# A two-layer decoder step on one core: prompt attention weights divided before their transposition, one search's counts split over two engines, and a reversed block order

## The reference, cut to what matters

```python
# mixer A: logits of the selected keys, softmax, values (16 heads of 64 in 2 groups)
logits = q @ k_sel * HEAD_DIM ** -0.5 + bias
p = softmax(where(dist >= 0, logits, NEG));  o = p @ v_sel
# mixer B: the sink joins the maximum and the sum, not the values
m = maximum(max(logits), sink);  e = exp(logits - m)
p = e / (sum(e) + exp(sink - m)); o = p @ v
```

## Time and profile before

| | us |
|---|---|
| median of 3 runs (lowest to highest) | 2345.16 (2342.01 to 2346.71) |
| the profiled execution, its own time | 2343.02 |
| its span in the profile | 2341.2 |
| mixer A's prompt attention, first logits to the first instruction of the samples | 131.89 |
| mixer B's prompt attention, the same | 80.70 |

### The profile page before, as it was taken

The page is one execution under the profiler, slowest core; times in us unless marked ns, Lnnn a source line. Parts: engine busy times, 40 slices in busy tenths (PEclk is TensorE's granted clock), DMA queues, the critical chain, the costliest instruction groups (busy, mean ns, idle before and its releaser), DMA issues.

```text
span 2341.2 us, 39794 instructions
## 1 busy us (share of the span) xinstructions
PE 2258.6 (96%) x14801; PEld 2029.8 (87%) x14819; DVE 1137.1 (49%) x1811; ACT 415.4 (18%) x848; POOL 1029.7 (44%) x622
## 2 busy tenths in 40 slices
PE   7999999999888899999999999999999999999997
PEld 6999989959666588999999999999996689999997
DVE  4544522488584546555512555542264465555311
ACT  3101000131554412010000101000015420101002
POOL 4546455414001024555555555555541055555552
PEclk9999999999799999999999999999999899999998
DMA  5435363535003433333223333322350023333221
GB/s 125 99 73 115 78 155 89 114 64 147 10 1 100 130 89 77 86 81 81 78 84 90 82 86 85 81 78 82 94 154 23 1 73 81 81 86 83 79 83 60
DMA packets 378042, 196.33 MB, mean 84 GB/s; under 512 B 66531, under 2 KB 374476, under 8 KB 377932
## 3 DMA queue, kind: packets, MB, share of 16 engines
q1 hardware_dynamic: 366108, 180.79, 31.3%
q10 hardware_dynamic: 11552, 13.71, 2.0%
q0 software_dynamic: 288, 0.56, 0.1%
HBM read 192.23 MB, written 11.64 MB: 87 GB/s over the span
## 4 chain that ended last, share of the span: by engine, by line
PE 61%; DVE 2%; ACTq 0%; ACT 0%; issue 0%; DVEq 0%
PE psum L594 17%; PE psum L597 11%; PE psum L595 10%; PE psum L593 10%; PE psum L596 9%; PE psum L749 1%; PE psum L775 1%; DVE XS L1448 1%; PE psum L745 1%; PE psum L789 1%; ACTq L1200 0%; PE psum L758 0%; DVE squares L1481 0%; PE psum L939 0%; PE psum L938 0%
## 5 line engine op out<-in xcount | busy, mean ns | idle before, releaser
L545 POOL CAST WSP<-WST 128x1024 fp32r<-128x1024 f32 (+1 forms) x305 | 310.5, 1018 | 1250.0 <-PE psum L597 1008.8
L547 POOL TENSOR_TENSOR WSP<-WST,WSP 128x1024 fp32r<-128x1024 f32 (+1 forms) x305 | 709.3, 2326 | 24.5
L594 PE MATMUL psum<-XS,WSP 128*128 128x512 f32 x1672 | 658.4, 394 | 0.0
L593 PE MATMUL psum<-XS,WSP 128*128 128x320 f32 x1672 | 520.4, 311 | 9.5 <-DVE XS L1448 4.3
L597 PE MATMUL psum<-XS,WSP 128*128 128x320 f32 x1672 | 522.7, 313 | 0.0
L595 PE MATMUL psum<-XS,WSP 128*128 128x320 f32 x1672 | 519.2, 311 | 0.0
L596 PE MATMUL psum<-XS,WSP 128*128 128x256 f32 x1672 | 474.0, 283 | 0.0
L596 PEld LDWEIGHTS psum<-XS,WSP 128*128 128x128 f32 x1672 | 314.8, 188 | 71.5
L593 PEld LDWEIGHTS psum<-XS,WSP 128*128 128x128 f32 x1672 | 321.4, 192 | 11.6 <-DVE XS L1448 5.2
L597 PEld LDWEIGHTS psum<-XS,WSP 128*128 128x128 f32 x1672 | 321.5, 192 | 0.0
L594 PEld LDWEIGHTS psum<-XS,WSP 128*128 128x128 f32 x1672 | 314.4, 188 | 0.4
(11 more groups left out here) (325 smaller groups left out, 2595.0 us busy)
## 6 DMA issues: line engine op xcount, KB each, us to landing
WST<-in_ffn_w_gate SPq DMA_DIRECT2D x168, 256.0 KB, 3.9
WST<-in_ffn_w_up SPq DMA_DIRECT2D x168, 256.0 KB, 3.9
WST<-in_ffn_w_down SPq DMA_DIRECT2D x192, 224.0 KB, 3.5
WST<-in_a_w_in SPq DMA_DIRECT2D x28, 256.0 KB, 4.4
kv0A<-in_cache_kv SPq DMA_DIRECT2D x48, 128.0 KB, 2.3
kv2A<-in_cache_kv SPq DMA_DIRECT2D x48, 128.0 KB, 2.3
WST<-in_b_w_in SPq DMA_DIRECT2D x20, 256.0 KB, 4.0
kscr<-in_cache_idx SPq DMA_DIRECT2D x128, 32.0 KB, 2.1
```

Source lines behind the costliest of these rows:

```text
L545: nc.gpsimd.tensor_copy(WSP[s][:, 0, 0:width], WST[s][:, 0:width]).then_inc(w_hi, 1)
L547: nc.gpsimd.tensor_tensor(WSP[s][:, 1, 0:width], WST[s][:, 0:width], WSP[s][:, 0, 0:width].bitcast(F32), ALU.subtract).then_inc(w_split, 1)
L593: mm(front, high, x[:, 0, 0:FRONT], start=first, stop=False)
L594: mm(split, high, x[:, :, FRONT:TOK], start=first, stop=False)
```

## The change

1. Both mixers: the weights are divided before T. VectorE's new `factors(u)` takes the reciprocal of the unit's two row sums and multiplies the weights in place, one instruction for each n; T waits for that (`pn_set`) and no longer for E. `row_scales`, `scales`, `products` and `otok` are gone. The high and low part come straight from the PSUM banks (`high_part` on ScalarE, `low_part` on VectorE).
2. TensorE's order in unit u was T(u), L(u+2), V(u-1); it is now L(u+2), V(u-1), T(u).
3. Mixer B: the sink is now a column of the bias strip (and a second column that holds the mask), so that maximum and sum take it in; strips are 258 wide for 256, and the four small sink instructions go.
4. Mixer A's blocks run 3, 2, 1, 0.
5. Of the counts beside the loop, those of even units below 24 are ScalarE's and the others VectorE's. Before, units 0 to 8 had ScalarE's and 9 to 23 VectorE's.
6. `block_diagonal` of mixer A goes from VectorE to GpSimd, ahead of its long wait; GpSimd's next weight split waits for the last `factors` (`pn_set`), before for the last logits. In the samples' part `new_logits` comes after three `keys`, and mixer B's samples wait for `ot_evac` later.

The core of the diff (the strips' widths, the removed buffers and names are left out):

```diff
@@ TensorE
-                for u, (r, i, g) in enumerate(units):
-                    more = u + 2 < len(units)
-                    transposed(u)
-                    if g == GRP - 1:
-                        row_scales(r, i)
-                    elif more:
-                        logits(u + 2)
-                    if u:
-                        values(u - 1)
-                    if g == GRP - 1 and more:
-                        logits(u + 2)
+                for u in range(len(units)):
+                    if u + 2 < len(units):
+                        logits(u + 2)
+                    if u:
+                        values(u - 1)
+                    transposed(u)
...
-                        pe.wait_ge(ms["p_set"], 2 * u + n + 1)
+                        pe.wait_ge(ms["pn_set"], 2 * u + n + 1)
@@ ScalarE
-                if FOUND + 1 + u <= SIGN_COUNTS:
+                if u in SIGN_UNITS:
                     count(FOUND + 1 + u)
...
+                    if g == 5:
+                        high_part(r, 0)
+                    if g == 1 and r:
+                        high_part(r - 1, 1)
@@ VectorE
+                def factors(u):
+                    r, i, g = units[u]
+                    dve.wait_ge(ms["p_set"], 2 * (u + 1))
+                    nc.vector.reciprocal(m["ri"][:, i, :, g], m["rs"][:, i, :, g]).then_inc(ms["ri_set"], 1)
+                    dve.wait_ge(ms["ri_set"], u + 1)
+                    for n in range(KVH):
+                        p = m["p"][:, u % 2, n, 0:key_range(L, i)[1]]
+                        ts(p, p, m["ri"][:, i, n, g:g + 1], None, ALU.mult).then_inc(ms["pn_set"], 1)
...
+                    nc.vector.tensor_reduce(m["nm"][:, i, :, g], PS[u % 2][:, :, 0:nk], AX, ALU.max, negate=True)\
+                        .then_inc(ms["nm_set"], 1)
+                    if u:
+                        factors(u - 1)
+                    if g == 7:
+                        low_part(r, 0)
                     if g == 3 and r:
-                        parts(r - 1)
+                        low_part(r - 1, 1)
                     after(u)
@@ constants
-ORDER = {"A": (0, 1, 2, 3), "B": (3, 2, 1, 0)}
-BITS, SIGN_COUNTS, FOUND = 32, 16, 7
+SINK = {"A": 0, "B": 2}
+STRIP = {L: 2 * P + SINK[L] for L in "AB"}
+ORDER = {"A": (3, 2, 1, 0), "B": (3, 2, 1, 0)}
+BITS, FOUND, SIGN_UNITS = 32, 7, range(0, 24, 2)
```

More of the change, by code:

```diff
@@ L557, in ffn, with block_diagonal @@
                         split(n0 + GU_CHUNKS + q, i, RING, DB * P)
+            def block_diagonal(m, ms):
+                pool.wait_ge(acc_evac, at["inA"][1] + A_CHUNKS + RING)
+                nc.gpsimd.memset(m["qbd"][:, :, :], 0.0).then_inc(ms["qbd_clear"], 1)
+                pool.wait_ge(ms["qbd_clear"], 1)
+                for n in range(KVH):
+                    h = slice(n * HD, (n + 1) * HD)
+                    dst = m["qbd"][h].rearrange("p b (n g t) -> p n g b t", n=KVH, g=GRP)[:, n]
+                    nc.gpsimd.tensor_copy(dst, m["qT"][h, :, SEQ:TOK].rearrange("p g (b t) -> p g b t", b=NB))\
+                        .then_inc(ms["qbd_set"], 1)
+                pool.wait_ge(ms["qbd_set"], KVH)
             ffn("ffn0")
@@ L569, in _ @@
                 .then_inc(MS["A"]["selb_in"], 16)
-            pool.wait_ge(MS["A"]["qk_ps"], NQT * GRP)
+            m, ms = mixers["A"], MS["A"]
+            block_diagonal(m, ms)
+            pool.wait_ge(MS["A"]["pn_set"], 2 * NQT * GRP)
             for t in range(ND):
@@ L751, in logits @@
                     ins.then_inc(ms["qk_ps"], 1)
[L753 to L761, removed]
                 turned = turned_counts(L)
@@ L883, in paged_sample_attention @@
                 keys(0, 2)
+                new_logits()
                 logits(0, 0)
@@ L1593, in prompt_attention @@
                         between(r)
-                    if g in (1, 2) and r:
-                        products(r - 1, (g - 1,))
-                    k0, nk = key_range(L, i)
+                    nk = key_range(L, i)[1] + SINK[L]
                     dve.wait_ge(ms["qk_ps"], u + 1)
-                    nm = m["nm"][:, i, :, g]
-                    ins = nc.vector.tensor_reduce(nm, PS[u % 2][:, :, 0:nk], AX, ALU.max, negate=True)
-                    if L == "B":
-                        steps.done(ins)
-                        ins = tt(nm, nm, m["nsink"][:, :, g], ALU.min)
-                    ins.then_inc(ms["nm_set"], 1)
-                    if L == "B" and g == GRP - 1:
-                        dve.wait_ge(ms["nm_set"], u + 1)
-                        if r:
-                            dve.wait_ge(ms["es_set"], r)
-                        tt(m["es"][:, :, :], m["nm"][:, i], m["nsink"][:, :, :], ALU.subtract).then_inc(ms["es_in"], 1)
-                    if g == 0 and r:
-                        row_scales(r - 1)
+                    nc.vector.tensor_reduce(m["nm"][:, i, :, g], PS[u % 2][:, :, 0:nk], AX, ALU.max, negate=True)\
[4 more added lines that the diff above has]
+                        low_part(r, 0)
                     if g == 3 and r:
-                        parts(r - 1)
+                        low_part(r - 1, 1)
                     after(u)
-                row_scales(NQT - 1)
-                products(NQT - 1, (0, 1))
-                parts(NQT - 1)
+                factors(len(units) - 1)
+                low_part(NQT - 1, 1)
             def paged_sample_attention(m, ms):
@@ L1906, in selections @@
                     sample_mask()
-                elif k == BITS + 2:
-                    block_diagonal(m, ms, a0 + A_CHUNKS)
             ranks = squares.rearrange("p a t -> p (a t)")[:, 0:SEGW]
@@ L2002 @@
 KV_SLOTS = 3
-ORDER = {"A": (0, 1, 2, 3), "B": (3, 2, 1, 0)}
-BITS, SIGN_COUNTS, FOUND = 32, 16, 7
+SINK = {"A": 0, "B": 2}
+STRIP = {L: 2 * P + SINK[L] for L in "AB"}
+ORDER = {"A": (3, 2, 1, 0), "B": (3, 2, 1, 0)}
+BITS, FOUND, SIGN_UNITS = 32, 7, range(0, 24, 2)
+SIGNED = (*range(1, FOUND + 1), *(FOUND + 1 + u for u in SIGN_UNITS))
 HALF_B = NB // 2
```

99 lines of the change are left out of this document (31 added, 68 removed).

## The result

The change makes the step slower: 2362.85 us (median of 4 runs, 2360.04 to 2367.29) against 2343.59 in the same comparison, a ratio of 1.0082 (95% interval 1.0061 to 1.0103), so 19 us more. The forecast was 2357, slower, with a range of 2341 to 2366. The two profiled executions, 2343.02 and 2360.04, lie 17.0 apart.

A forecast was written before the change was run, and what follows sets the result against it. The prediction took mixer A as bound by its search's chain, mixer B by TensorE. Circle and ends +9, clock +14, mixer B -10 gave +13 on 2343.0, so 2356; forecast 2357, between two readings, range 2341 to 2366.

The forecast's parts named there:

- The circle: Mixer A's search: a closed chain of waits through VectorE, TensorE and ScalarE sets each pair's period, 10.9 us at 512 keys.
- D: Mixer A's search: VectorE's decision, which needs ScalarE's count of the even unit; 0.82 us of the pair's period.
- C: Mixer A's search: VectorE's own count, behind its decision; 1.22 us of the pair's period at 512 keys.
- division to T: Mixer A's search: reciprocal, first product and signal until the transposition can start; 0.7 us at 512 keys.
- K to the shuffle: Mixer A's search: from ScalarE's count to VectorE's decision, which the shuffle starts; 1.30 us.
- The tail of mixer A: End of mixer A's loop: 14.6 us to the selection's end, then 10.2 for five short units, drain and low clock.
- up to the first shuffle: Start of mixer A's loop, first logits to first alternating decision: 8.6 us plus 1.7 for the low clock, 10.3.
- the search's clock: Mixer A's twelve pairs: TensorE's clock falls after its one long wait, 1.2 us each, +14; bounds 0 and 20.
- Mixer B: Mixer B's loop: TensorE stays the bound; removed spreads, waits and end products save 10 us, bounds 8 to 12.
- The rest: Outside the two loops: GpSimd's moved work hides and the second sample's page load stays covered; 0 us.
- Rival 1: Mixer A: TensorE's clock stays up between pairs, so +9 - 10 = -1, 2344 us; chance 0.18.
- Rival 2: Mixer A: TensorE bounds the loop, pairs of 8.1, 6.5 and 5.0 us, whole -33, 2312 us; chance 0.07.

The follow-up runs named there:

- experiment 1: Changed kernel with 20 unread identity transpositions filling TensorE's wait in each of mixer A's odd units 1 to 23: 2347.7 us, 1.0021 of the kernel before.
- experiment 2: Changed kernel with ScalarE's count moved ahead of the copy of the transposed weights, behind the next unit's exponentials: 2332.7 us, 0.9959 of the kernel before.
- experiment 3: Changed kernel with all counts beside mixer A's loop on VectorE, none on ScalarE: 2330.1 us, 0.9940 of the kernel before.
- experiment 4: Changed kernel with all 24 counts beside mixer A's loop on ScalarE: 2361.0 us, 1.0072 of the kernel before.
- experiment 5: Changed kernel with ScalarE's count put ahead of the next unit's exponentials: 2320.2 us, 0.9907 of the kernel before.
- experiment 9: Changed kernel with only the alternation undone, ScalarE counting in units 0 to 8 and VectorE in 9 to 23: 2341.4 us, 0.9989 of the kernel before.
- Experiment 8: The kernel of experiment 5 with 16 identity transpositions ahead of TensorE's wait in mixer A's units 24 to 26: 2314.4 us, 0.9877 of the kernel before.
- the second profile: Changed kernel run again, unchanged, and profiled: 2360.8 us, 1.0083 of the kernel before; mixer A's loop 161.81 us.
- experiment 10: Changed kernel with TensorE's old order, transposition first, in mixer B alone: 2386.2 us, 1.0190 of the kernel before.

## Why the forecast held, and what in it was off

**The circle: right.** Forecast 10.9, 9.6 and 8.3 a pair. Undisturbed pairs: 10.95, 9.57, 8.37 (experiment 1). Forecast for the eleven periods 105.7, measured 104.56. Its pieces: D 0.82, C 1.21, division to T 0.73 for 0.7, K to the shuffle 1.29. The product that the trace of before did not show takes 0.48 at 512 keys, nearer to the cast that I took (0.42) than to the upper bound (0.69). Experiments 2, 3, 4, 5 and 9 each open or close the circle at another place, and the length follows each time.

**The tail of mixer A: the step that failed.** I gave the end 24.8: 14.6 for the selection and 10.2 for the last short units, with 1.7 for a low clock. Measured are 14.88 and 14.70. The selection was right; the short units ran at half clock to the very end, 2.72 apart where I took 1.6:

```profile
736.85 0.69 PE L775 MATMUL psum<-ident,pA 128*128 128x128 f32 x2
...
739.57 0.69 PE L775 MATMUL psum<-ident,pA 128*128 128x128 f32 x2
```

Experiment 8 keeps the clock at 0.86 there and gets 24.87. So the tail is 4.8 longer than my sum, 4.5 of it in the short units. Term by term the loop has 10.9 for 10.3 up to the first shuffle, 104.6 for 105.7 in the circle, 9.9 for 14 in the search's clock and 29.6 for 24.8 in the tail: +0.6, -1.1, -4.1 and +4.8. They cancel. That 154.9 was hit to the tenth is chance, and the second profile has 161.8.

**Mixer B: right sign, 2 too much.** Forecast -10, bounds 8 to 12, measured -8.15, and 72.2 to 73.0 in all eleven profiles with this loop. The removed spreads are gone from TensorE's queue; no run restores them alone, so their share is worked out and not measured by itself. What I left out is the price of T as the last of a unit: at the start the third logits wait 0.55 for the exponentials, and at the end, with no logits left between a copy and its values, V waits three times:

```profile
1854.32 0.44 PE L789 MATMUL psum<-ptB,kvtokB 128*64 128x128 f32 x4 [0.53 <-ACT ptB L1235]
...
1855.78 0.44 PE L789 MATMUL psum<-ptB,kvtokB 128*64 128x128 f32 x4 [0.66 <-ACT ptB L1235]
...
1857.18 0.69 PE L789 MATMUL psum<-ptB,kvtokB 128*64 128x128 f32 x4 [0.53 <-ACT ptB L1235]
1857.80 1.97 PE L907 MATMUL psum<-ident,kvB 128*128 128x128 f32 x8
```

That is 1.7 at the end and 0.6 at the start, more than the 1.85 that are missing.

**The rest: put at 0, measured +2.1.** The 3.8 of mixer B's samples are clock (0.57 against 0.77). The samples' instructions take 21.5 to 25.8 us in the eleven profiles with this loop, so the size differs from one execution to the next. But the fall itself seems to come with the change. In nine of the eleven the clock has fallen by the last V, behind the three waits above (0.69 for 0.44), and the samples' first eight transpositions take 1.97. In the other two, experiments 3 and 5, they take 1.09; this is experiment 3's row:

```profile
1831.02 1.09 PE L907 MATMUL psum<-ident,kvB 128*128 128x128 f32 x8
```

They take 1.09 also in both profiles in which T stands first in mixer B: the kernel before, with samples of 21.95, and experiment 10, with 21.79. So the waits that the new order leaves at the loop's end are the likely cause. With two profiles of the old order, and no run that fills these waits, it is not shown.

**The sum.** +13 forecast; +23.0 - 8.2 + 2.1 = 17 in the profiled execution. Rival 1 (the clock stays up, 2344) is what experiment 1 brings about in the search, and it gives 2347.7, above 2344 in the main because the tail stays long. The clock is what makes the change clearly slower, the circle what makes it no gain. Rival 2 (TensorE bounds A, 2312) is what the order of instructions in experiment 5 allows, 2320.

## What to carry to other kernels

When work is put on the path between two engines, follow each wait through the queues until it comes back to where it began: a sum of loads per engine says nothing of such a circle. Here one moved call on ScalarE, with no work removed, was worth 2361 to 2320 us. When an engine's wait is long and in one piece, ask what its clock does behind it, and look at the last, short units too, where it stayed low to the end here.

## What the runs showed of the hardware that I had not expected

- More idle time in shorter pieces can leave TensorE's clock higher. Waits of 1.6 to 2.0 us in every unit of 512 and 384 keys, a third of the time, left it at 1.00 (experiment 4). Waits of 2.3 to 3.2 in every second unit, with TensorE idle for 29% of the search, brought it to 0.89, and for 27% in the second execution to 0.83. It is no rule: in experiment 4's units of 256 keys, with waits up to 2.3 us, the clock was 0.82.
- The same kernel's loop differed by 7 us between two profiled executions (154.93 and 161.81) although T's waits for the products summed to 38.3 and 38.4 us in them: the granted clock was 0.81 and 0.77. The whole differed by 1.6.
- In mixer B three waits of 0.53 to 0.66 us at the loop's end stood ahead of a fall to half clock in nine of eleven profiles.
- Twenty transpositions in each of twelve waits, whose output nobody reads, made the kernel some 14 us faster.
